# Running sums of the first modulation in PSUM, low parts of the input tiles on GpSimd, six products beside the input tiles instead of seven

## What is computed

```python
mod = c @ w_ada[layer] + b_ada[layer]
sh_a, sc_a, gt_a, sh_m, sc_m, gt_m = jnp.split(mod, 6, axis=-1)

h = modulate(rmsnorm(x, g_mix[layer]), sh_a, sc_a)
z = h @ w_in[layer]
(zq, zkc, zvc, zks, zvs, zkw, zvw, zg, zqd, zkvd, zkr, zga, zgb) = jnp.split(z, split_points, axis=-1)
```

## Time and profile before

| | us |
|---|---|
| median of 3 runs | 2195.74 |
| the runs | 2191.86 to 2201.43 |
| the profiled execution, its own time | 2193.43 |
| its span in the trace | 2191.6 |
| PE busy | 2060.2 |
| DVE busy | 1171.4 |
| ACT busy | 787.9 |
| POOL busy | 742.7 |

### The profile page before, as it was taken

How to read it: one execution, slowest core, us unless ns; L and a number is a source line. 1 busy time by engine, 2 the same in 40 slices (tenths; PEclk the granted TensorE clock), 3 DMA queues, 4 the chain that set the end, 5 groups by cost and what they waited for, 6 DMA issues and landing times. The chain is left out here.

```text
span 2191.6 us, 35961 instructions
## 1 busy us (share of the span) xinstructions
PE 2060.2 (94%) x14840; PEld 1622.3 (74%) x14840; DVE 1171.4 (53%) x1863; ACT 787.9 (36%) x1300; POOL 742.7 (34%) x355
## 2 busy tenths in 40 slices
PE   4998989998999999989999999999999998999997
PEld 3875667877788888767777777776777786888886
DVE  7536675332752342736678667767713457524322
ACT  3446655222432232443333333333333434323321
POOL 4210021434344444452232133123233443344442
PEclk8989999999899999999999999999999999999998
DMA  7421012532433333331111111111122332333331
GB/s 279 171 84 40 11 49 87 189 99 87 137 110 95 101 96 96 94 108 33 36 43 47 36 35 46 44 31 45 45 93 95 125 96 76 95 98 96 96 96 68
DMA packets 53041, 186.89 MB, mean 85 GB/s; under 512 B 6032, under 2 KB 7184, under 8 KB 52624
## 3 DMA queue, kind: packets, MB, share of 16 engines
q1 hardware_dynamic: 49104, 174.49, 25.5%
q10 hardware_dynamic: 3776, 10.09, 1.3%
HBM read 178.27 MB, written 6.29 MB: 84 GB/s over the span
## 5 line engine op out<-in xcount | busy, mean ns | idle before, releaser
L756 POOL TENSOR_TENSOR wlo<-raw,whi 128x1024 fp32r<-128x1024 f32 x261 | 632.1, 2422 | 1245.7 <-ACT whi L1401 1245.7
L842 PE MATMUL psum<-ah,whi 128*128 128x512 f32 x1248 | 522.0, 418 | 32.3 <-DVE ah L1829 18.2
L843 PE MATMUL psum<-ah,whi 128*128 128x512 f32 x1248 | 495.9, 397 | 0.0
L844 PE MATMUL psum<-ah,wlo 128*128 128x512 f32 x1248 | 494.9, 397 | 0.0
L1401 ACT ACTIVATE whi<-raw 128x1024 fp32r<-128x1024 f32 x261 | 274.7, 1053 | 306.8 <-PE psum L844 295.0
L842 PEld LDWEIGHTS psum<-ah,whi 128*128 128x128 f32 x1248 | 239.1, 192 | 103.8 <-POOL wlo L756 16.7
L844 PEld LDWEIGHTS psum<-ah,wlo 128*128 128x128 f32 x1248 | 239.4, 192 | 52.7
L843 PEld LDWEIGHTS psum<-ah,whi 128*128 128x128 f32 x1248 | 239.9, 192 | 41.8 <-issue 0.2
L2152 DVE SCALAR_TENSOR_TENSOR x<-upad,vec,x 128x512 f32<-128x512 f32 x240 | 210.7, 878 | 5.1
L842 PE MATMUL psum<-hidden,whi 128*128 128x512 f32 x536 | 210.0, 392 | 0.1
L843 PE MATMUL psum<-hidden,whi 128*128 128x512 f32 x536 | 209.3, 391 | 0.0
(11 more groups left out here) (357 smaller groups left out, 2939.0 us busy)
## 6 DMA issues: line engine op xcount, KB each, us to landing
raw<-in_w SPq DMA_DIRECT2D x300, 512.0 KB, 3.6
raw_first<-in_w SPq DMA_DIRECT2D x14, 512.0 KB, 7.7
raw_ck<-in_w SPq DMA_DIRECT2D x8, 512.0 KB, 7.1
x<-in_x SPq DMA_DIRECT2D x4, 512.0 KB, 6.0
x_kept<-x ACTq DMA_DIRECT2D x1, 2048.0 KB, 7.7
ao_kept<-ao ACTq DMA_DIRECT2D x8, 256.0 KB, 2.0
aof<-ao_kept ACTq DMA_DIRECT2D x1, 2048.0 KB, 12.3
x<-x_kept ACTq DMA_DIRECT2D x1, 2048.0 KB, 8.5
```

Source lines behind the costliest of these rows:

```text
L756: pool.tensor_tensor(lo_weight(place(s)), raw_of(SPLITS[s]), hi_weight(place(s)).bitcast(F32), ALU.subtract).then_inc(lo_done, 1)
L842: pe.matmul(dst, wh, h_, start=first, stop=False)
L843: pe.matmul(dst, wh, l_, start=False, stop=False)
L844: return pe.matmul(dst, wl, h_, start=False, stop=last)
```

## The change

Five things, all in the first 90 us of the program:

1. The running sum of a tile's modulation lies in PSUM (columns 256 to 511 of bank 7) for k = 0 to 6; the last step writes it to `mod_sum` in SBUF, where PE reads it.
2. What `sum_mod` writes goes to a bank of the common order, under the new name `("mods",)`, which is third in `bank_order()`.
3. The low part of the eight input tiles is made on POOL (a subtraction of 128 x 512) instead of on DVE. The multiplication of the tiles 0 and 1 by the inverse root goes from POOL to DVE, which reads it from PSUM; POOL keeps the tiles 2 to 7.
4. POOL's order is new: two weight blocks first, then for each tile its low part, the multiplication of the tile two further, and a weight block.
5. `AHEAD` has six products; z 15 is now the first entry of `FRONT`, and its weights take one of the two places that turn.

```diff
--- before.py
+++ after.py
@@ -74,8 +74,8 @@
 
-AHEAD = [("z", 11), ("z", 4), ("z", 12), ("z", 5), ("z", 13), ("z", 14), ("z", 15)]
-FRONT = [("z", 10), ("bkv", 0), ("z", 7), ("bkv", 1), ("ck", 0, 0), ("ss", "cq"), ("ck", 0, 1), ("z", 9), ("root", "cq"), ("ck", 0, 2), ("ck", 0, 3),
+AHEAD = [("z", 11), ("z", 4), ("z", 12), ("z", 5), ("z", 13), ("z", 14)]
+FRONT = [("z", 15), ("z", 10), ("bkv", 0), ("z", 7), ("bkv", 1), ("ck", 0, 0), ("ss", "cq"), ("ck", 0, 1), ("z", 9), ("root", "cq"), ("ck", 0, 2), ("ck", 0, 3),
          ("z", 6), ("norm", "cq"), ("ck", 1, 0), ("ck", 1, 1), ("ck", 1, 2), ("z", 8), ("kc",), ("ck", 1, 3), ("gt",), ("vt", 0), ("vt", 1),
          ("ss", "ckv"), ("z", 0), ("root", "ckv"), ("vc",), ("norm", "ckv")]
 INSIDE = [("z", 1), ("z", 2), ("z", 3)]
@@ -306,7 +306,7 @@
 
 def bank_order():
-    out = [("ss", "mix"), ("rb", "mix")] + AHEAD
+    out = [("ss", "mix"), ("rb", "mix"), ("mods",)] + AHEAD
     for f in FRONT:
         if f[0] == "ck":
             if f[2] == CK_PARTS - 1:
@@ -616,7 +616,8 @@
         x_loaded = [sem(f"x_loaded{i}") for i in range(KT // 2)]
         vec_loaded, vec_rest_loaded = sem("vec_loaded"), sem("vec_rest_loaded")
-        mod_taken, mod_summed, mod_ready, x_scaled = sem("mod_taken"), sem("mod_summed"), sem("mod_ready"), sem("x_scaled")
+        mod_taken, mod_summed, mod_ready = sem("mod_taken"), sem("mod_summed"), sem("mod_ready")
+        x_first, x_scaled = sem("x_first"), sem("x_scaled")
         const_loaded = {n: sem(f"{n}_loaded") for n in CONSTS}
         w_loaded = [sem(f"w_loaded{i}") for i in range(NRAW + RAW_FIRST + RAW_CK)]
         raw_used = sem("raw_used")
@@ -756,10 +757,15 @@
                     pool.tensor_tensor(lo_weight(place(s)), raw_of(SPLITS[s]), hi_weight(place(s)).bitcast(F32), ALU.subtract).then_inc(lo_done, 1)
                     low[0] += 1
+            weights_ahead(1)
             wait_emptied(pool, ("rb", "mix"))
             for m in range(KT):
-                pool.tensor_tensor(spread_x[m], x[:, m, :], sq_sum[:, 1, :], ALU.mult).then_inc(x_scaled, 1)
-                weights_ahead(min(m, len(AHEAD) - 1))
+                e = EVENT["mix", m]
+                pool.wait_ge(hi_ready, e + 1)
+                pool.tensor_tensor(ah[:, 1, m, :], tmp[:, e % NTMP, :], ah[:, 0, m, :].bitcast(F32), ALU.subtract).then_inc(hl_ready, 1)
+                if m + 2 < KT:
+                    pool.tensor_tensor(spread_x[m + 2], x[:, m + 2, :], sq_sum[:, 1, :], ALU.mult).then_inc(x_scaled, 1)
+                weights_ahead(min(m + 2, len(AHEAD) - 1))
             weights_ahead(SPLIT_AT["rkv", 0, 1] - 1)
             weights_ahead(SPLIT_AT["rkv", 0, 1] + 1)
@@ -1027,9 +1033,16 @@
             def sum_mod(m):
                 pe.wait_ge(mod_taken, KT * m + KT)
+                if m == 0:
+                    free(("mods",))
                 for i in range(2):
-                    mm = pe.matmul(psum[:, OBANK, 2 * m + i:2 * m + i + 1], mod_sum[m % 2][:, i * P:i * P + P], ones[:, 0:1], start=True, stop=True)
-                mm.then_inc(mod_summed, 1)
+                    mm = pe.matmul(bank(("mods",))[:, 2 * m + i:2 * m + i + 1], mod_sum[m % 2][:, i * P:i * P + P], ones[:, 0:1], start=True, stop=True)
+                if m < KT - 1:
+                    mm.then_inc(mod_summed, 1)
+                else:
+                    assert FILL["mods",] == fills[0]
+                    fills[0] += 1
+                    mm.then_inc(filled, 1)
             def ahead(e, k):
@@ -1443,13 +1456,18 @@
             act.activation(rs[:, 2 * TT:2 * TT + 1], ones[:, 0:1], ACT.Sqrt)
             squares("mix", x, lambda k: act.wait_ge(x_loaded[k // 2], 16))
             root("mix")
-            weights_ahead(0)
+            weights_ahead(1)
+            act.wait_ge(x_first, 2)
             empty(("rb", "mix"), sq_sum[:, 1, :])
-            weights_ahead(1)
             for m in range(KT):
                 n = EVENT["mix", m]
-                act.wait_ge(x_scaled, m + 1)
-                act.wait_ge(mod_ready, 2 * m + 2)
+                if m >= 2:
+                    act.wait_ge(x_scaled, m - 1)
+                if m < KT - 1:
+                    act.wait_ge(mod_ready, 2 * m + 2)
+                else:
+                    act.wait_ge(mod_ready, 2 * m + 1)
+                    wait_emptied(act, ("mods",))
                 if n >= NTMP:
                     act.wait_ge(hl_ready, n - NTMP + 1)
                 act.activation(tmp[:, n % NTMP, :], spread_x[m], ACT.Identity, bias=mod[:, m:m + 1], scale=modg[:, m:m + 1]).then_inc(pre_split, 1)
@@ -1876,23 +1894,31 @@
                 if k % 4 == 0:
                     wait_loaded(dve, ("mod", m, k // 4))
-                w, total = raw_of(("mod", m, k // 4))[:, k % 4 * 2 * P:k % 4 * 2 * P + 2 * P], mod_sum[m % 2]
+                w, total = raw_of(("mod", m, k // 4))[:, k % 4 * 2 * P:k % 4 * 2 * P + 2 * P], psum[:, OBANK, S // 2:S // 2 + 2 * P]
+                if k == KT - 1 and m >= 2:
+                    dve.wait_ge(mod_summed, m - 1)
+                if m or k:
+                    dve.wait_ge(mod_taken, KT * m + k)
                 if k == 0:
-                    if m >= 2:
-                        dve.wait_ge(mod_summed, m - 1)
                     ins = dve.tensor_scalar(total, w, vcol("c", k), None, ALU.mult)
                 else:
-                    dve.wait_ge(mod_taken, KT * m + k)
-                    ins = dve.scalar_tensor_tensor(total, w, vcol("c", k), total, ALU.mult, ALU.add)
+                    into = mod_sum[m % 2] if k == KT - 1 else total
+                    ins = dve.scalar_tensor_tensor(into, w, vcol("c", k), total, ALU.mult, ALU.add)
                 ins.then_inc(mod_taken, 1)
             def mod_tile(m):
-                dve.wait_ge(mod_summed, m + 1)
-                both = psum[:, OBANK, 2 * m:2 * m + 2]
+                if m < KT - 1:
+                    dve.wait_ge(mod_summed, m + 1)
+                else:
+                    wait_filled(dve, ("mods",))
+                both = bank(("mods",))[:, 2 * m:2 * m + 2]
                 dve.tensor_tensor(mod[:, m:m + 1], both[:, 0:1], vcol("b_ada", m), ALU.add).then_inc(mod_ready, 1)
-                dve.scalar_tensor_tensor(modg[:, m:m + 1], both[:, 1:2], mod[:, KT + m:KT + m + 1], vcol("g_mix", m), ALU.add,
-                                         ALU.mult).then_inc(mod_ready, 1)
+                ins = dve.scalar_tensor_tensor(modg[:, m:m + 1], both[:, 1:2], mod[:, KT + m:KT + m + 1], vcol("g_mix", m), ALU.add, ALU.mult)
+                if m < KT - 1:
+                    ins.then_inc(mod_ready, 1)
+                else:
+                    emptied_by(ins, ("mods",))
             for k in range(1, KT):
                 add_square("mix", k)
@@ -1905,17 +1931,14 @@
                     inverse_root("mix")
                 take_mod(0, k)
             for m in range(KT):
-                if m == 0:
-                    mod_tile(m)
-                for k in range(KT if m + 1 < KT else 0):
-                    take_mod(m + 1, k)
-                    if m and k == 1:
+                for k in range(KT if m + 1 < KT else 2):
+                    if m + 1 < KT:
+                        take_mod(m + 1, k)
+                    if m == 0 and k < 2:
+                        wait_filled(dve, ("rb", "mix"))
+                        dve.tensor_tensor(spread_x[k], x[:, k, :], bank(("rb", "mix")), ALU.mult).then_inc(x_first, 1)
+                    if k == 1:
                         mod_tile(m)
-                    if k == 4:
-                        low(("mix", m), ah[:, 0, m, :], ah[:, 1, m, :])
-                if m == KT - 1:
-                    mod_tile(m)
-                    low(("mix", m), ah[:, 0, m, :], ah[:, 1, m, :])
             dve.wait_ge(vec_rest_loaded, 16)
             for f in FRONT:
                 kind = f[0]
```

## The result

Over six runs each, the changed kernel takes 2184.34 us in the median (2181.28 to 2186.5) and the kernel before 2196.26 (2191.77 to 2202.54). The ratio is 0.9943, 95% interval 0.9929 to 0.9956: 12 us or 0.57% faster. The interval lies clear of no change at all, but it reaches from 0.44% to 0.71% and so isn't clear of the 0.5% that was taken as the least gain one can tell. The prediction was 2186.5. The profiled execution took 2182.76 us with a span of 2181.0.

A forecast was written before the change was run, and what follows sets the result against it. DVE was taken to bound the first 70 us, though PE is busy for 2060 of 2192 us. -11.3 (walk) + 2.1 (attention) = -9.2 on 2193.4 gives 2184.2; the median stands 2.3 higher: 2186.5, range 2180 to 2194.

The forecast's parts named there:

- The step in PSUM: DVE's running sum: a step with its sum in PSUM takes 0.52 us, as before, and doesn't wait for POOL.
- The rival in which the steps are held all the same: DVE's steps in PSUM are still held, by POOL or the PSUM write; 1.2 us slower, 2196.9; chance 0.06.
- The round trip: In the walk, from sum_mod on PE over DVE, ACT and POOL's low part to a ready tile: 3.8 us.
- s1: Start of sum_mod for tile 1 on PE, forecast at 26.5 us; s2 to s7 are those of later tiles.
- mark: First matmul of z 10 on PE, behind all walking products: from 89.14 to 76.3 us, or 77.9 with low clock.
- The term that was mis-sized: PE's low clock in the walk, through m=2 and the start of m=3: 1.6 us charged, at most 2.8.
- my 2.7 and 2.45: The six slow PE matmuls of tile 0 and those of tile 1 at the walk's start, in us.
- The attention's bank: At the attention's start, first scores wait for bank 0, now used by the spread of ckv: 2.1 us lost.
- The low parts on POOL: In the walk, POOL's subtraction takes 1.29 us where DVE's takes 0.69: 0.6 us more in each round trip.
- The other edits at nothing: Ninth bank entry, z 15 in FRONT, a later modulation's step leaving the attention, the wait for ("mods",): no cost or gain.
- The sum: Whole kernel: 11.3 us gained in the walk less 2.1 lost at the attention, -9.2 us.
- the same: Verdict that the kernel's time differs by less than about 0.5%, 11 us: chance 0.66, against 0.31 faster and 0.03 slower.

The follow-up runs named there:

- e1: The changed kernel with the running sums back in SBUF and all else as changed: 2196.6 us.
- e7: The kernel before with running sums in PSUM, the bank ("mods",) and a walk of six; DVE, ACT and POOL lists in their old order: 2183.43 us.
- e6: The changed kernel with ten further matmuls, whose result nobody reads, on PE ahead of the walk: 2182.84 us.
- e4: The changed kernel with the attention's turn of banks begun at bank 1 instead of 0: 2180.6 us.
- e2: The changed kernel with the low parts of the eight input tiles back on DVE: 2180.0 us.
- e3: The kernel before with six products walking along instead of seven, nothing else changed: 2195.22 us.
- e5: The changed kernel with low parts on DVE again and the attention's banks dealt out from the second: 2175.3 us.
- e8: The changed kernel with low parts on DVE, the attention's banks from the second, and ten further matmuls ahead of the walk: 2174.53 us.

## Why the prediction was right, point by point

**The step in PSUM** (0.52 us, no wait for POOL; bounds 0.52 to 0.96). Right: 0.53 in a row of five, 490 ns at the median where it was 485, 491 at most. The Trainium skill (VectorE: DVE Perf Modes, the TRN2 errata) led to an estimate of 65 ns more a step; this trace shows 5, and the last steps, which read PSUM and write SBUF, take 479 to 482 ns, so the measurement decides against it here. The first step of a tile, which only writes PSUM, went from 0.35 to 0.49 us, once a tile, on an engine that now has time.

**The rival in which the steps are held all the same** fell with that, and e1 with e7 show the step is the source: without it 2196.6, with it and the walk of six alone 2183.4. The Trainium skill (SBUF — State Buffer, Who interferes with whom) says that DVE contends with GpSimd's reads when it has two inputs in SBUF, and with at most one doesn't, outside of its two-port modes; by that rule, 2451 ns with the sum in SBUF (e1's longest) against 491, the trace agrees. Another rival, that the loads hold the steps, is ruled out by the kernel before, where three steps beside POOL's work take 4.47 us for the free 1.5, while the DMA share is 0.05 (60 to 66 us):

```profile
59.88 4.47 DVE L1886 SCALAR_TENSOR_TENSOR mod_sums<-raw_first,vec,mod_sums 128x256 f32<-128x256 f32 x3
60.27 2.40 POOL L756 TENSOR_TENSOR w_ahead<-raw_first,w_ahead 128x1024 fp32r<-128x1024 f32 x1 [3.86 <-ACT w_ahead L1401]
62.63 1.44 POOL L761 TENSOR_TENSOR kwd<-x,sq_sum 128x512 f32<-128x512 f32 x1
```

**The round trip**, for the changed kernel in us:

```
                    s1     s2     s3     s4     s5     s6     s7    m=7    z 15   mark
predicted          26.5   32.7   39.0   44.2   50.1   57.3   62.5   66.3   70.8   76.3 (+1.6)
measured           25.75  32.53  38.17  43.46  49.41  56.72  62.01  66.06  70.76  76.29
```

The walk's first matmul was forecast at 23.8 and came at 23.05, 0.6 of it by the chance at the start. With these 0.6 taken off, every entry is right to 0.6 or better; the mark came 0.6 later than worked out so, and only the chance makes 76.3 and 76.29 agree. The order is as forecast, and the handing over of z 15's weights came as worked out (0.32 us for 0.4). The round trip of 3.8 us was 4.1 while sum_mod ran at the low clock, 3.8 for the tiles 3 and 6 (38.17 to 41.97, 56.72 to 60.51) and 4.05 for tile 7 (62.01 to 66.06), whose low part on POOL took 1.45 us instead of 1.28.

**The term that was mis-sized** is the low clock in the walk. I charged 1.6 us to it beyond tile 1, by the 0.64 before. It cost nothing there: tile 1's later matmuls stand 0.23 apart from 33.56 on, and the windows from 40 to 90 us are at 1.00. What the low clock did cost lay in tiles 0 and 1, in my 2.7 and 2.45 (both took 2.7), and e6 prices it at 2.8. A loss of the same size that I had not charged came at 120 to 140 us:

```profile
120.00:130.00 10.00, 8.65 (x59) 7.83 (x58) 1.88 (x1) 6.05 (x13) 1.40 (x2) 0.94 0.41 148
130.00:140.00 10.00, 9.28 (x36) 7.25 (x36) 0.16 (x1) 1.23 (x2) 1.76 (x1) 0.72 0.18 52
```

The kernel before had 1.00 in both of these, and 0.83 from 140 to 150. The lead was still 12.86 at a weight block of ACT (128.27 against 141.13) and 11.26 at the spread of ckv. That the clock did it is supported by e4, which had 1.00 and 0.83 in these windows: its spread came 12.61 earlier than before, with a lead at the mark of 12.60.

**The attention's bank** (2.1 us, bounds 0 to 3.7). The mechanism and the place were right, 3.15 us of standing for 3 forecast, and 1.85 lost for 2.1 (from 11.26 to 9.41). e4 confirms it by taking 1.65 of it away.

**The low parts on POOL** (0.6 us a round trip). Right in size, but I never summed it: over the walk it made 3.8 us (e2), where the whole change brought 12.85 at the mark. The sum hid it inside "3.8 us from sum_mod to the tile".

**The other edits at nothing.** For the walk of six e3 bears that out, with the sums in SBUF. The rest have no run of their own; between the mark and 128 us the lead doesn't move, so nothing there cost or gained.

**The sum.** -9.2 forecast; -9.4 behind the attention's transposes. This closeness is in part luck: the 1.6 us of low clock that I charged in the walk weren't lost there, 1.6 that I hadn't charged were lost from 128 us on, and the 0.6 of chance at the start covers the 0.6 by which the walk took longer. The mechanism, sums freed from POOL and then a bounded round trip, is what the runs show. The profiled execution ended 10.6 us below the old one, so 1.2 us more came later, over a list that is the same. Profiles of these kernels differ there by 3 us and more in either direction (e5's lead goes from 14.3 at 250 us to 21.1 at 1500 and back to 18.1), so I give it no cause. The medians are 11.9 apart, more than the 9.2 forecast. The measured 0.57% lies just outside of 0.5%, but its interval, 0.44% to 0.71%, reaches to both sides, so the result counts as "the same", on which 0.66 stood.

## What to carry to other kernels

Look for an engine whose instructions of one shape differ by a factor of five: its longest ones show what it shares, and moving one operand to another memory can be the whole gain (the sum's move to PSUM shifted the mark by some 13 us in e7, as much as the whole change did). Sum a cost per round trip over all round trips before accepting it, above all when the work leaves an engine that the same change has just unloaded: the low parts may have belonged on POOL as long as DVE was last, but no run shows that. When an entry is added to a rotation of buffers, follow which later pair of uses now falls on the same one; here one number gave 1.65 us back at the attention.

## What the runs showed that I had not expected

- A DVE step with one tensor input in SBUF and its output in SBUF, TENSOR_SCALAR of 128x256, took 0.35 us alone and 2.23 us beside POOL's block of 2.54 us (e1, 21.36 and 28.54). So one tensor input in SBUF is not enough to be safe from POOL. The Trainium skill (SBUF — State Buffer, Who interferes with whom) makes this exception for a mode of this instruction that uses both ports, and the row agrees. With its output in PSUM the instruction took 0.49 us and was not held.
- POOL is slowed as well. Its weight block took 2.36 us beside steps in PSUM and 2.54 beside steps in SBUF, its multiplication 1.28 and 1.46 (changed kernel and e1, the blocks at 30.95 and 28.08).
- Ten idle matmuls before the walk brought its first products to the full clock, and in e8 PE was back at the low clock for tile 1 (27.42 on, 0.50 from 28 to 32 us), after standing for 2.61 us; in e6 it stood for 3.23 us and kept the full one (1.00 in the same stretch). How long it stood doesn't tell the two apart.
